# A float32 network on one core: stage ends by halves, a diagonal product in place of scale and transpose, high parts first

## The reference

```
# first block, for each layer
h = rms_norm(x, g0);  h = time_mix(h) or attention(h);   x = x + rms_norm(h, g1)
h = conv_ffn(rms_norm(x, g2));                           x = x + rms_norm(h, g3)
# second block, for each layer
x = x + mixer(rms_norm(x, mix_g))
x = x + square(relu(rms_norm(x, mlp_g) @ w1)) @ w2

rms_norm(x, g) = x * rsqrt(mean(x*x, -1) + 1e-6) * g
```

## Time and profile before

| what | value |
|---|---|
| runs | 1416.57 us median of 3 (1416.51 to 1419.28) |
| profiled execution | 1415.92 us, span 1414.2 us |
| PE busy | 1342.9 us, 95% of the span |
| PEld busy | 1211.0 us, 86% |
| DVE busy | 935.9 us, 66% |
| ACT busy | 742.6 us, 53% |
| granted TensorE clock | 0.984 of full over the span |
| DMA | 222.30 MB, mean 157 GB/s |

### The profile page before, as it was taken

The page is one execution under the profiler, slowest core; times in us unless marked ns, Lnnn a source line. Parts: engine busy times, 40 slices in busy tenths (PEclk is TensorE's granted clock), DMA queues, the critical chain, the costliest instruction groups (busy, mean ns, idle before and its releaser), DMA issues.

```text
span 1414.2 us, 26104 instructions
## 1 busy us (share of the span) xinstructions
PE 1342.9 (95%) x10471; PEld 1211.0 (86%) x10471; DVE 935.9 (66%) x1362; ACT 742.6 (53%) x1155; POOL 47.2 (3%) x89
## 2 busy tenths in 40 slices
PE   7999988999989889999989999999999998999998
PEld 6878877999978869999968987999987877899997
DVE  7988876777776756777764667555556756555554
ACT  5854226555565655555564635444444654544443
POOL 6000001000000000000000000100001000000000
PEclk9999999999999989999999999999999999999999
DMA  9511038555554127555636544556554550355550
GB/s 275 184 52 33 19 96 284 188 178 178 183 175 149 60 91 264 181 178 180 202 126 201 183 142 159 179 185 195 184 179 149 179 179 1 122 190 195 178 178 31
DMA packets 136844, 222.30 MB, mean 157 GB/s; under 512 B 6281, under 2 KB 107889, under 8 KB 136496
## 3 DMA queue, kind: packets, MB, share of 16 engines
q1 hardware_dynamic: 134464, 214.32, 46.5%
q0 software_dynamic: 2144, 6.61, 1.5%
q10 hardware_dynamic: 144, 0.06, 0.0%
HBM read 219.90 MB, written 1.05 MB: 156 GB/s over the span
## 4 chain that ended last, share of the span: by engine, by line
PE 87%; DVE 7%; ACT 3%; issue 2%; DMA 0%; ACTq 0%; DVEq 0%
PE ps L512 84%; PE ps L838 1%; DVE ulo L498 1%; DVE x_sb L1948 1%; DVE xn_lo L1936 1%; DVE scratch L2377 0%; ACT uhi L490 0%; PE ps L1219 0%; DVE xs L1924 0%; ACT scratch L1447 0%; DMA scratch<-in_mu 0%; DVE x_sb L1954 0%; ACT xn_hi L1478 0%; PE ps L1015 0%; DVE scratch L1981 0%
## 5 line engine op out<-in xcount | busy, mean ns | idle before, releaser
L498 DVE TENSOR_TENSOR ulo<-raw,uhi 128x1024 fp32r<-128x1024 f32 x395 | 482.3, 1225 | 352.9 <-ACT uhi L490 352.3
L490 ACT ACTIVATE uhi<-raw 128x1024 fp32r<-128x1024 f32 x395 | 417.6, 1060 | 418.5 <-PE ps L512 417.6
L512 PE MATMUL ps<-xn_hi,uhi 128*128 128x256 f32 x1472 | 418.2, 284 | 2.2 <-DVE xn_lo L1936 1.7
L512 PE MATMUL ps<-xn_lo,uhi 128*128 128x256 f32 x1472 | 416.7, 283 | 0.0
L512 PE MATMUL ps<-xn_hi,ulo 128*128 128x256 f32 x1472 | 416.6, 283 | 0.0
L512 PEld LDWEIGHTS ps<-xn_hi,uhi 128*128 128x128 f32 x1472 | 282.6, 192 | 5.8 <-issue 1.9
L512 PEld LDWEIGHTS ps<-xn_lo,uhi 128*128 128x128 f32 x1472 | 282.6, 192 | 1.7
L512 PEld LDWEIGHTS ps<-xn_hi,ulo 128*128 128x128 f32 x1472 | 282.5, 192 | 0.0
L512 PE MATMUL ps<-uhi,xm_hi 128*128 128x512 f32 x512 | 200.5, 392 | 2.9 <-DVE xm_lo L2325 1.1
L512 PE MATMUL ps<-ulo,xm_hi 128*128 128x512 f32 x512 | 199.9, 391 | 0.0
L512 PE MATMUL ps<-uhi,xm_lo 128*128 128x512 f32 x512 | 159.1, 389 | 0.0
(11 more groups left out here) (295 smaller groups left out, 1261.3 us busy)
## 6 DMA issues: line engine op xcount, KB each, us to landing
raw<-in_mlp_w SPq DMA_DIRECT2D x64, 1024.0 KB, 5.3
raw<-in_w_up SPq DMA_DIRECT2D x44, 1024.0 KB, 5.1
raw<-in_w_down SPq DMA_DIRECT2D x22, 1024.0 KB, 4.9
raw<-in_gmlp_w_in SPq DMA_DIRECT2D x16, 1024.0 KB, 5.3
raw<-in_fox_w_in SPq DMA_DIRECT2D x16, 1024.0 KB, 5.2
raw<-in_w_rkv SPq DMA_DIRECT2D x12, 1024.0 KB, 6.2
raw<-in_gmlp_w_out SPq DMA_DIRECT2D x8, 1024.0 KB, 4.9
raw<-in_w_q SPq DMA_DIRECT2D x4, 1024.0 KB, 5.3
```

What stands on the lines that cost most here:

```text
L490: nc.scalar.activation(ring_unit(uhi, m, n), raw_unit(n, j), ACT.Copy).then_inc(hi_done, 1)
L498: nc.vector.tensor_tensor(ring_unit(ulo, m, n), raw_unit(n, j), ring_unit(uhi, m, n).bitcast(F32), ALU.subtract).then_inc(lo_done, 1)
L512: return nc.tensor.matmul(o, l, r, start=start, stop=stop, skip_group_check=True)
```

## The change

The last pair of units of a stage is taken by tok and by column half, and each of the first three quarters signals `half_ps`. The squares of the output norm are taken per half as each is there, the small addition of epsilon goes from ACT to DVE, and tok 1 of x is written in two halves (`x_half`, `x_ready`), each squared by itself. DVE no longer scales x: it scales the identity by the reciprocals (`scale_diag`, 128 by 128, in `xs`), and PE multiplies the unscaled `x_sb` by that diagonal, an ordinary float32 product in place of a transpose. The first unit of the next stage makes all products with the high part of x first and then those with the low part (`u_unit_first`, and the same by unit for `d_unit` with `n0` and for kvd). The split of the second weight unit moves from ahead of the copies into their middle, ahead of bank 2, on ACT and on DVE; the loading of the Gelu table on ACT moves from ahead of the copies to behind them. The output is stored in three DMAs in place of two.

```diff
+        def u_unit_first(pe, m, o, mhi, mlo, n0, hi_split, lo_split):
+            pe.wait_ge(lo_done, m + 1)
+            wh, wl = (b[:, m % RING, :].rearrange("p (k c) -> p k c", c=128) for b in (uhi, ulo))
+            for k in range(NF):
+                pe.wait_ge(hi_split, n0 + k + 1)
+                mm(o, wh[:, k, :], mhi[:, k, :], k == 0, False)
+                mm(o, wl[:, k, :], mhi[:, k, :], False, False)
+            for k in range(NF):
+                pe.wait_ge(lo_split, n0 + k + 1)
+                last = mm(o, wh[:, k, :], mlo[:, k, :], False, k == NF - 1)
+            return last.then_inc(unit_done, 1)
...
         def d_last_pair(pe, m, lhi, llo, base=0):
+            def products(tok, j, half, final):
+                t, c = slice(P * tok, P * tok + P), slice(512 * half, 512 * half + 512)
+                wh, wl = uhi[:, (m + j) % RING, c], ulo[:, (m + j) % RING, c]
+                mm(acc(tok, half, base), lhi[:, j, t], wh, False, False)
+                mm(acc(tok, half, base), lhi[:, j, t], wl, False, False)
+                return mm(acc(tok, half, base), llo[:, j, t], wh, False, final)
+            for half in range(2):
+                for j in range(2):
+                    if half == 0:
+                        pe.wait_ge(lo_done, m + j + 1)
+                    last = products(0, j, half, j == 1)
+                last.then_inc(half_ps, 1)
+            for half in range(2):
+                last = products(1, 0, half, False)
+            last.then_inc(unit_done, 1)
+            for half in range(2):
+                products(1, 1, half, True).then_inc((half_ps, unit_done)[half], 1)
...
-            def norm(n, e):
+            def norm(n):
                 for tok in range(NT):
-                    pe.wait_ge(xs_done, 3 * n + tok + 1)
+                    pe.wait_ge(xs_done, NT * n + tok + 1)
                     for b in range(4):
-                        if tok == 1 and b == 2:
-                            pe.wait_ge(xs_done, 3 * n + 3)
                         for f in range(2):
                             c = (2 * b + f) * P
-                            last = nc.tensor.transpose(bank(b, P, T * f + P * tok), xs[:, tok, c:c + P], ident[:, :])
+                            last = mm(bank(b, P, T * f + P * tok), x_sb[:, tok, c:c + P], scale_diag(tok), True, True)
...
-            def boundary(n, nxt_units, k=None, base=0, then=None):
+            def boundary(n, nxt_units, k=None, base=0):
                 warm(ACT.Sqrt)
                 if k is not None:
-                    act.wait_ge(tok_ps, n)
-                    out_rms(k, 0, base)
-                    upto(nxt_units + 2)
+                    for half in range(2):
+                        act.wait_ge(half_ps, 3 * n - 2 + half)
+                        out_squares(k, 0, half, base)
+                    out_root(k, 0)
+                    act.wait_ge(half_ps, 3 * n)
+                    out_squares(k, 1, 0, base)
                     act.wait_ge(unit_done, nxt_units)
-                    out_rms(k, 1, base)
+                    out_squares(k, 1, 1, base)
+                    out_root(k, 1)
                 act.wait_ge(x_tok, n)
                 rms(n, 0)
-                upto(nxt_units + 2)
-                act.wait_ge(x_ready, n)
-                rms(n, 1)
-                if then is not None:
-                    warm(then)
+                rms_halves(n)
-            def split_x(s, e, g, dst=xn_hi):
+            def split_x(s, e, g, dst=xn_hi, nxt_units=None):
                 for b in range(4):
+                    if b == 2 and nxt_units is not None:
+                        upto(nxt_units + 2)
                     act.wait_ge(tr_done, 4 * e + b + 1)
...
-            def norm(n, nxt_units=None):
+            def norm(n):
                 for tok in range(NT):
+                    if tok == 1 and n > 0:
+                        dve.wait_ge(sum_done, n)
+                        TS(stat[:, 6:7], stat[:, 1:2], RMS_EPS, None, ALU.add).then_inc(eps_done, 1)
                     dve.wait_ge(rms_done, NT * n + tok + 1)
                     step(nc.vector.reciprocal(stat[:, 4 + tok:5 + tok], stat[:, 2 + tok:3 + tok]))
-                    for c in ((slice(0, D),), (slice(0, D // 2), slice(D // 2, D)))[tok]:
-                        TS(xs[:, tok, c], x_sb[:, tok, c], stat[:, 4 + tok:5 + tok], None, ALU.mult).then_inc(xs_done, 1)
-                if nxt_units is not None:
-                    upto(nxt_units + 2)
+                    TS(scale_diag(tok), ident[:, :], stat[:, 4 + tok:5 + tok], None, ALU.mult).then_inc(xs_done, 1)
...
             def add_out(n, nxt_units, base=0):
-                for tok, (s, v) in enumerate(((tok_ps, n), (unit_done, nxt_units))):
+                for tok, half, s, v, done in ((0, None, half_ps, 3 * n - 1, x_tok), (1, 0, half_ps, 3 * n, x_half),
+                                              (1, 1, unit_done, nxt_units, x_ready)):
                     dve.wait_ge(s, v)
-                    TT(x_sb[:, tok, :], x_sb[:, tok, :], acc(tok, base=base), ALU.add)\
-                        .then_inc((x_tok, x_ready)[tok], 1)
+                    c = slice(0, D) if half is None else slice(512 * half, 512 * half + 512)
+                    TT(x_sb[:, tok, c], x_sb[:, tok, c], acc(tok, half, base), ALU.add).then_inc(done, 1)
```

More of the change, by code:

```diff
@@ L197, in col, with scale_diag @@
             return vec[:, c:c + 1]
+        def scale_diag(tok):
+            return xs[:, tok, 0:P]
         def f3(ap):
@@ L537, in d_unit @@
                     mm(acc(tok, half, base), lhi[:, t], wl[:, c], False, False)
-                for half in range(2):
-                    c = slice(512 * half, 512 * half + 512)
-                    last = mm(acc(tok, half, base), llo[:, t], wh[:, c], False, final)
+                if n0 is None:
+                    for half in range(2):
+                        c = slice(512 * half, 512 * half + 512)
+                        last = mm(acc(tok, half, base), llo[:, t], wh[:, c], False, final)
@@ L541, in d_unit @@
+            if n0 is not None:
+                pe.wait_ge(xlo_done, n0)
+                for tok in range(NT):
+                    t = slice(P * tok, P * tok + P)
+                    for half in range(2):
+                        c = slice(512 * half, 512 * half + 512)
+                        last = mm(acc(tok, half, base), llo[:, t], wh[:, c], False, final)
             return last.then_inc(unit_done, 1)
         def d_last_pair(pe, m, lhi, llo, base=0):
-            for tok in range(NT):
-                t = slice(P * tok, P * tok + P)
+            def products(tok, j, half, final):
[4 more added lines that the diff above has]
+                return mm(acc(tok, half, base), llo[:, j, t], wh, False, final)
@@ L564, in d_gemm @@
+                last.then_inc(half_ps, 1)
+            for half in range(2):
+                last = products(1, 0, half, False)
+            last.then_inc(unit_done, 1)
+            for half in range(2):
+                products(1, 1, half, True).then_inc((half_ps, unit_done)[half], 1)
+        def d_gemm(pe, name, lhi, llo, nk=NF, base=0, before=None, by_token=False, n0=None):
             m0 = unit0(at[name])
@@ L1129, in up @@
                         for j in range(2):
-                            u_unit(pe, m + 2 * part + j, bank(4 + 2 * (p % 2) + part, T, T * j),
-                                   xn_hi, xn_lo, i, split if p == 0 and part == 0 and j == 0 else None)
+                            o = bank(4 + 2 * (p % 2) + part, T, T * j)
+                            if p == 0 and part == 0 and j == 0:
+                                u_unit_first(pe, m, o, xn_hi, xn_lo, split, xhi_done, xlo_done)
+                            else:
+                                u_unit(pe, m + 2 * part + j, o, xn_hi, xn_lo, i)
                 def down(q, i=None):
@@ L1173, in _ @@
                         mm(o, xm_hi[:, k, t], wl[:, j, :], False, False)
-                        last = mm(o, xm_lo[:, k, t], wh[:, j, :], False, k == NF - 1)
+                for j in range(2):
+                    k = 2 * e + j
+                    pe.wait_ge(xlo_done, 8 * 2 + k + 1)
+                    for tok in range(NT):
+                        last = mm(bank(4 + tok), xm_lo[:, k, P * tok:P * tok + P], wh[:, j, :], False, k == NF - 1)
                 last.then_inc(unit_done, 1)
@@ L1940, in out_norm @@
                 dve.wait_ge(gb_in[row], 16 * loads)
-                for tok, (s, v) in enumerate(((tok_ps, n), (unit_done, nxt_units))):
-                    dve.wait_ge(s, v)
-                    TT(xs[:, tok, 512:1024], acc(tok, 1, base), gb[:, row, 512:1024], ALU.mult).then_inc(hg_half, 1)
-                    dve.wait_ge(hsq_done, NT * (NT * k + tok) + 1)
-                    step(TT(xs[:, tok, 0:512], acc(tok, 0, base), gb[:, row, 0:512], ALU.mult))
+                for tok in range(NT):
+                    for half in range(2):
+                        dve.wait_ge(hsq_done, 4 * k + 2 * tok + half + 1)
```

(10 more changed lines are left out.)

164 lines of the change are left out of this document (89 added, 75 removed).

## The result

The changed kernel took 1427.89 us (median of 5 runs, 1426.81 to 1432.27) against 1416.51 before, 11.4 us more. The ratio to the kernel before is 1.0086, with a 95% interval from 1.0071 to 1.0100. 1423.8 was forecast, with a range up to 1427.5: the sign was right, the size a third too small, and the time lies just outside the range. The profiled execution took 1426.81 (span 1424.9; before 1415.92 and 1414.2).

What follows compares the result with a forecast made beforehand. The chain runs 87% through PE, with time open at the eight stage ends. Start +1.0, ends 1 to 8 +0.95, +2.25, +1.75, +0.7, +0.55, +0.6, 0, -0.6: together +7.2, 1423.8 us, range 1415.5 to 1427.5.

Steps and rivals of the forecast that it cites:

- Idle ahead of the diagonal products: Stage ends: PE's idle falls from 4.97 to 3.7 once and 4.4 three times, from 2.18 to 1.2 three times.
- the rival that had PE wait as long as before: Stage ends: tok 0's diagonal waits for something other than DVE's order, PE still idles 4.97; 1427, chance 0.04.
- The price of a product: Diagonal products on PE: 0.22 each at full clock, 0.44 at half, against 0.117 and 0.23 per transpose.
- c: ACT's copies start, counted from PE's last product: 7.5 at end 1, 8.3 at ends 2 to 4, 3.55 at 5 to 7.
- half clock throughout: Rival: clock down from first diagonal product into unit 1 at ends 1 to 4; +9.7, 1426.3, chance 0.13.
- full clock: Rival: the clock stays up at ends 1 to 4, c at 6.0 and 6.7; +0.9, 1417.5, chance 0.25.
- The reading of rows 5: Granted-clock rows before the change: transposes alone brought the clock back to 1.00, against the skill's rule that they don't count.
- The tails: From c to PE's second unit: 5.65 where it was 4.81 or 4.64; 0.85 longer at ends 1 and 3, 1.0 at 5 and 7.
- the wait at gv that was to be over 1 us: End 4: PE newly waits over 1 us for the third unit, ready at c + 8.0; the end +0.7.
- My rival that had the split in the middle off the path: Seven stage ends: DVE's split between low parts isn't on the path, tails 0.3 shorter; about -5.7, 1410.9, chance 0.08.
- The step that failed, at kvd: End 2: third unit at c + 9.8 instead of c + 8.4, +1.35; the end +2.25 in all.
- Start and end: Program start +1.0 from dearer products (bounds +0.3 to +1.6); last stage end -0.6 from DVE's smaller last addition.

Runs made afterwards that it cites:

- one look: One of two profiled executions of the changed kernel, the second run with the experiments; timed beside the kernel before, the changed kernel measured 1.0086, and again 1.0088.
- The experiment that takes it away: Changed kernel with kvd's third weight unit split ahead of the second norm's copies and the mixer's last pair unit by unit for token block 0: 1.0050.

## Why the direction was right and the size wrong

- *Idle ahead of the diagonal products:* 3.60, 4.14, 4.14 and 4.51, 1.18 three times, against 3.7, 4.4 three times and 1.2. The scaled identity took 0.29 on DVE where 0.25 was taken. Right, and the rival that had PE wait as long as before is out.
- *The price of a product:* 32 records take 3.84 at full clock; less the last one's latency (0.28) and by 16 that is 0.22, and eight transposes take 1.09, 0.117 each. The Trainium skill (TensorE: Matmul & The Clock Gate, Terms) has a factor of four for the transpose mode; the measurement says two, and decides.
- *c:* forecast 7.5, 8.3, 8.3, 8.3; 8.27, 7.79, 8.81, 8.67 in one look, 7.77, 8.30, 8.17, 9.19 in the other: 1.1 too little over four ends. The clock is at half for most of the products, and where it comes back differs from run to run. Summed over the four ends, c was 33.5 and 33.4 in the two looks, between my middle (32.4) and the rival "half clock throughout" (34.9); the rival "full clock" (6.0 and 6.7) is out. The reading of rows 5 holds: in the kernel before, the granted clock is 0.50 in 427.00 to 427.40 and 1.00 in 427.60 to 427.95, with PE still at its transposes and its next product at 428.97, so transposes alone brought the clock back.
- *The tails:* 5.75 and 5.62 against 5.65; kvd's third unit c + 9.79 against 9.8, gv's 7.76 against 8.0, fk's 9.05 against 9.2. Right, but the wait at gv that was to be over 1 us is 0.92 and 0.31. My rival that had the split in the middle off the path is out.
- *The step that failed, at kvd:* I priced the longer wait ahead of the third unit by its own length (+1.35) and took PE's work behind it at full clock. The wait of 2.5 put PE to half clock behind it, 24 products in 7.19 where 5.59 were needed: 1.6 more. Since c came 0.5 sooner than forecast in that look, 1.1 of it is left in the ledger. fk is the same case (a wait of 2.19, forecast as an addition to the way alone): no fall in the first look, a fall in the second, +2.22.
- *The step that was missing:* "halves" reorder PE's last pair of units as well, so that the last unit is needed 3 products sooner. In the mixer its split isn't ready, +0.7. I had followed the reordering behind T only, never ahead of it. The experiment that takes it away gives it back.
- *Start and end:* the start was over-priced in the first look (+0.29 for +1.0) and not in the second (+1.36); the last end gives 1.19 where 0.6 was forecast. DVE's last addition ends 0.54 sooner behind PE's last product, as priced; the last store lands 2.03 after its issue where the one of twice the size took 2.65, and this the forecast had put at nothing.
- *Not the change's:* +1.31 in q and attention, whose instructions are untouched. This stretch measures 82.8 to 85.5 over the 17 traces of this study (82.85 before, 84.16 after). It takes 82.8 to 83.0 where the granted clock in it is 0.98, 84.0 to 84.5 at 0.96 and 85.5 at 0.94, and the same kernel with filling products had 82.95 in one look and 84.10 in the other. So 1.3 of the miss in the spans is chance.

Forecast and measured spans differ by 3.5: kvd 1.1, attention 1.3, ends 1 and 3 1.5, mixer 0.7, ends 4 to 7 0.6, less 0.7 at the start, 0.6 at the end and 0.4 in the other stretches.

## What to carry to other kernels

Price a wait on TensorE with the clock behind it, not by its length alone: here a wait of about two us in front of gapless products cost 1.6 on top, more often than not. Work moved off an idle stretch onto the chain costs its whole length; both engines had 1.9 us or more free ahead of the copies, and moving the split there gave the whole loss of that edit back. When an order of products changes to finish one half sooner, look also at what its operands' producers must deliver sooner.

## What the runs showed of the hardware

The waits of PE ahead of the third unit, in kvd and fk, over all 17 traces, and whether the granted clock was half behind it. The 0.07, 0.57 and 0.97 of kvd stand ahead of the fourth unit, in the kernels that split the third one sooner; at fk one trace has no wait.

```
kvd, no fall:  0.07 0.57 0.80 0.81 0.82 0.97 1.43 1.76 1.77   2.85
kvd, fall:     1.89 2.06 2.14 2.15 2.50 2.83 2.85
fk, no fall:   0.17 0.19 0.22 0.60 1.03 1.03 1.50 1.54 1.54   2.00 2.19 2.19
fk, fall:      2.19 2.19 2.19 2.22
```
None of 18 waits of up to 1.77 was followed by the lower clock; 11 of 15 of 1.89 to 2.85 were, and the same kernel went either way (2.85 twice at kvd; 2.19 at fk in the changed kernel). The idle stretches ahead of the transposes or diagonal products at ends 5 to 7 show no sharp edge either: the clock fell by the end of unit 1 in none of 21 with 1.18 idle, in 1 of 15 with 1.64 (the old order of products, end 5) and in 11 of 15 with 2.18, among them the sixth and seventh end of the kernel before and not its fifth. What decides in one kernel stays open. Products whose result nobody uses, put into the idle stretch, held the clock at full through the transposes or diagonal products behind them in all 24 stage ends where they stood (six traces); the transposes, in three of these traces, ran at 0.117 each. At the same four ends without them it fell in all 44 (eleven traces).
